# Rotary step: the exchanged halves copied by ScalarE, one VectorE operation fewer

## The reference, cut to what matters

```python
def _rope(x, pos):
    ang = pos[:, None] * inv[None, :]
    x1, x2 = x[..., :half], x[..., half:]
    return concatenate([x1 * cos - x2 * sin, x2 * cos + x1 * sin])
```

## Time and profile before

| what | value |
|---|---|
| median of 3 runs | 2270.43 us (2269.36 to 2271.97) |
| profiled execution | 2269.12 us, its span 2267.3 us |
| busy: TensorE, VectorE, ScalarE, GpSimd | 2232.9, 1803.7, 984.7, 990.3 us |
| attention halves, P k0 to the last output tile | from 40, 285.5, 1163 and 1400.3 us; 218.4, 209.2, 210.0 and 209.2 us long |
| feed-forward stretches | about 500 to 1145 and 1615 to 2250 us |

### The profile page before, as it was taken

One profiled execution on the slowest core, in us unless ns is written; L12 is line 12 of the kernel. 1 busy time (PEld: TensorE's weight loads), 2 busy tenths in 40 slices (PEclk: granted clock), 3 DMA queues, 4 the chain that ended last, 5 costly groups with the idle time before them and its releaser, 6 DMA issues.

```text
span 2267.3 us, 31231 instructions
## 1 busy us (share of the span) xinstructions
PE 2232.9 (98%) x10610; PEld 1858.7 (82%) x10610; DVE 1803.7 (80%) x2793; ACT 984.7 (43%) x1876; POOL 990.3 (44%) x686
## 2 busy tenths in 40 slices
PE   8999999999999999999999999999999999999998
PEld 6888888888888888888888888888888888888886
DVE  7998388888787878999958873988877676779988
ACT  4556144554444444443324541455444434444342
POOL 4314100124777777798700010001254455568893
PEclk9999999999999999999999999999999999999999
DMA  8633542233676766853243136312323232357522
GB/s 306 221 111 124 205 174 94 83 141 117 215 239 215 236 216 235 316 175 108 99 149 112 56 130 214 121 59 110 135 84 111 97 111 97 111 212 261 165 72 84
DMA packets 93463, 346.89 MB, mean 153 GB/s; under 512 B 9760, under 2 KB 9888, under 8 KB 74016
## 3 DMA queue, kind: packets, MB, share of 16 engines
q1 hardware_dynamic: 92624, 344.53, 43.7%
q10 hardware_dynamic: 720, 0.86, 0.1%
HBM read 237.35 MB, written 108.00 MB: 152 GB/s over the span
## 4 chain that ended last, share of the span: by engine, by line
PE 87%; DVE 6%; issue 1%; ACT 1%; POOL 0%; DVEq 0%; ACTq 0%; POOLq 0%
PE bank L528 28%; PE bank L530 27%; PE bank L529 27%; PE bank L1177 2%; PE bank L1015 1%; DVE x L2234 1%; DVE u L2200 1%; PE bank L1023 1%; PE bank L535 1%; PE bank L534 1%; DVE qpe L1928 1%; DVE aT_lo L2053 1%; DVE y_out L2341 0%; ACT aT_hi L1490 0%; DVE x L2242 0%
## 5 line engine op out<-in xcount | busy, mean ns | idle before, releaser
L905 POOL TENSOR_TENSOR slot<-raw,slot 128x512 fp32r<-128x512 f32 x160 | 223.4, 1400 | 234.4 <-ACT slot L1629 234.4
L528 PE MATMUL bank<-h_hi,slot 128*128 128x512 f32 x640 | 249.2, 389 | 0.0
L529 PE MATMUL bank<-h_lo,slot 128*128 128x512 f32 x640 | 249.1, 389 | 0.0
L530 PE MATMUL bank<-h_hi,slot 128*128 128x512 f32 x640 | 249.1, 389 | 0.0
L882 POOL TENSOR_TENSOR acc<-sq,zero 128x512 f32<-128x512 f32 x5 | 6.1, 1219 | 528.3 <-ACT sq L1418 528.3
L528 PE MATMUL bank<-u,slot 128*128 128x512 f32 x560 | 218.6, 390 | 1.1 <-DVE x L2234 1.1
L529 PE MATMUL bank<-u,slot 128*128 128x512 f32 x560 | 218.1, 389 | 0.0
L530 PE MATMUL bank<-u,slot 128*128 128x512 f32 x560 | 218.0, 389 | 0.0
L528 PE MATMUL bank<-h_hi,w 128*128 128x512 f32 x512 | 203.6, 398 | 0.0
L905 POOL TENSOR_TENSOR slot<-s_stage,slot 128x512 fp32r<-128x512 f32 x120 | 175.8, 1466 | 60.1 <-ACT slot L1629 58.6
L530 PE MATMUL bank<-h_hi,w 128*128 128x512 f32 x512 | 200.0, 391 | 0.0
(11 more groups left out here) (261 smaller groups left out, 5931.6 us busy)
## 6 DMA issues: line engine op xcount, KB each, us to landing
w<-parked SPq DMA_DIRECT2D x81, 1024.0 KB, 4.9
raw<-in_wffn SPq DMA_DIRECT2D x112, 512.0 KB, 3.5
u_kept<-made SPq DMA_DIRECT2D x148, 256.0 KB, 2.8
uf<-u_kept SPq DMA_DIRECT2D x70, 512.0 KB, 5.7
parked<-w SPq DMA_DIRECT2D x27, 1024.0 KB, 6.3
parked<-p SPq DMA_DIRECT2D x27, 1024.0 KB, 4.9
raw<-in_watt SPq DMA_DIRECT2D x27, 512.0 KB, 4.3
praw<-in_watt SPq DMA_DIRECT2D x27, 512.0 KB, 5.8
```

The source lines that it names most:

```text
L528: nc.tensor.matmul(out_ap, lhs[0], rhs[0], start=first, stop=False, skip_group_check=joins)
L529: nc.tensor.matmul(out_ap, lhs[0], rhs[1], start=False, stop=False, skip_group_check=joins)
L530: return nc.tensor.matmul(out_ap, lhs[1], rhs[0], start=False, stop=last, skip_group_check=joins)
L905: nc.gpsimd.tensor_tensor(slot[i][:, 1, :], gate_source(i), slot[i][:, 0, :].bitcast(F32), ALU.subtract).then_inc(s_gate_lo.sem, 1)
```

## The change

ScalarE gets a new item RS x in its order, which copies the two 64-partition halves of the projected tile from PSUM into the other halves of r2. It waits for the projection of the tile and for the end of the rotary step before it. VectorE waits for both copies, multiplies by the cosine table, multiplies all of r2 by the sine rows in place, and subtracts (the sine rows of partitions 64 to 127 hold the negative, so the sign changes). The bank counts as read after that product.

```diff
 SCALAR_ORDER = order("""
-    V | RH q0 | RH k0 | EX 0 | EX 1 | RH q1 | TH 0 | EX 2 | TH 1 | RH k1 | EX 3 | TH 2 | EX 4 | RH q2 | EX 5 | TH 3 |
-    YC 0 | TH 4 | RH k2 | EX 6 | RH q3 | TH 5 | EX 7 | TH 6 | EX 8 | RH k3 | TH 7 | EX 9 | EX 10 | SH y0 | TH 8 |
...
+    V | RS q0 | RH q0 | RS k0 | RH k0 | RS q1 | EX 0 | EX 1 | RH q1 | TH 0 | EX 2 | RS k1 | TH 1 | RH k1 | EX 3 |
+    RS q2 | TH 2 | EX 4 | RH q2 | EX 5 | TH 3 | YC 0 | RS k2 | TH 4 | RH k2 | EX 6 | RS q3 | RH q3 | TH 5 | EX 7 |
+    RS k3 | TH 6 | EX 8 | RH k3 | TH 7 | EX 9 | RS kpe | EX 10 | SH y0 | TH 8 | YC 1 | TH 9 | EX 11 | LC ckv | TH 10 |
...
+    PH kn0 | TH 14 | RS pe0 | PH qn0 | TH 15 | RH pe0 | EX 16 | PH vm0 | PH vm1 | PH vm2 | YC 3 | PH vm3 | PH kn1 |
+    SH y2 | EX 17 | TH 16 | PH qn1 | EX 18 | EX 19 | SQ 0 | PH kn2 | SQ 1 | TH 17 | SH y3 | EX 20 | RS pe1 | SQ 2 |
...
+            def swap_halves(l, b, name):
+                z = bank[TILE[name] % 2]
+                act.wait_ge(s_mm.sem, s_mm.half_at(l, b, DV_MM + TILE[name]))
+                act.wait_ge(s_roped.sem, s_roped.half_at(l, b, ROPED[name] - 1))
+                nc.scalar.activation(r2[0:64, :], z[64:128, :], ACT.Copy).then_inc(s_swapped.sem, 1)
+                nc.scalar.activation(r2[64:128, :], z[0:64, :], ACT.Copy).then_inc(s_swapped.sem, 1)
...
+                dve.wait_ge(s_swapped.sem, s_swapped.half_at(l, b, 2 * ROPED[name] + 1))
                 nc.vector.tensor_tensor(r1[:], z[:], tab[:, 0, :], ALU.mult)
-                nc.vector.tensor_tensor(r2[0:64, :], z[64:128, :], tab[64:128, 1, :], ALU.mult)
-                nc.vector.tensor_tensor(r2[64:128, :], z[0:64, :], tab[0:64, 1, :], ALU.mult).then_inc(s_rope_read.sem, 1)
+                nc.vector.tensor_tensor(r2[:], r2[:], tab[:, 1, :], ALU.mult).then_inc(s_rope_read.sem, 1)
                 dve.wait_ge(s_rope_read.sem, s_rope_read.half_at(l, b, ROPED[name]))
-                nc.vector.tensor_tensor(r1[:], r1[:], r2[:], ALU.add).then_inc(s_roped.sem, 1)
+                nc.vector.tensor_tensor(r1[:], r1[:], r2[:], ALU.subtract).then_inc(s_roped.sem, 1)
```

More of the change, by code:

```diff
@@ L83 @@
 SCALAR_ORDER = order("""
-    V | RH q0 | RH k0 | EX 0 | EX 1 | RH q1 | TH 0 | EX 2 | TH 1 | RH k1 | EX 3 | TH 2 | EX 4 | RH q2 | EX 5 | TH 3 |
-    YC 0 | TH 4 | RH k2 | EX 6 | RH q3 | TH 5 | EX 7 | TH 6 | EX 8 | RH k3 | TH 7 | EX 9 | EX 10 | SH y0 | TH 8 |
[L86 to L92, removed]
+    V | RS q0 | RH q0 | RS k0 | RH k0 | RS q1 | EX 0 | EX 1 | RH q1 | TH 0 | EX 2 | RS k1 | TH 1 | RH k1 | EX 3 |
+    RS q2 | TH 2 | EX 4 | RH q2 | EX 5 | TH 3 | YC 0 | RS k2 | TH 4 | RH k2 | EX 6 | RS q3 | RH q3 | TH 5 | EX 7 |
+    RS k3 | TH 6 | EX 8 | RH k3 | TH 7 | EX 9 | RS kpe | EX 10 | SH y0 | TH 8 | YC 1 | TH 9 | EX 11 | LC ckv | TH 10 |
+    EX 12 | RH kpe | SH y1 | TH 11 | EX 13 | EX 14 | SH ckv | LC cq0 | LC cq1 | TH 12 | EX 15 | TH 13 | SH cq | YC 2 |
+    PH kn0 | TH 14 | RS pe0 | PH qn0 | TH 15 | RH pe0 | EX 16 | PH vm0 | PH vm1 | PH vm2 | YC 3 | PH vm3 | PH kn1 |
+    SH y2 | EX 17 | TH 16 | PH qn1 | EX 18 | EX 19 | SQ 0 | PH kn2 | SQ 1 | TH 17 | SH y3 | EX 20 | RS pe1 | SQ 2 |
+    TH 18 | PH qn2 | RH pe1 | PH kn3 | EX 21 | TH 19 | PH qn3 | EX 22 | EX 23 | EX 24 | TH 20 | YC 4 | EX 25 | EX 26 |
+    TH 21 | TH 22 | EX 27 | TH 23 | TH 24 | SQ 3 | SQ 4 | YC 5 | TH 25 | EX 28 | TH 26 | EX 29 | EX 30 | SQ 5 | SQ 6 |
+    TH 27 | SQ 7 | SN 0 | TH 28 | SN 1 | SN 2 | TH 29 | EX 31 | SN 3 | SN 4 | SN 5 | TH 30 | YC 6 | TH 31 | YC 7 |
+    SN 6 | SN 7
 """)
@@ L456, in encoder_trunk @@
         s_roped = Count(sem("roped"), len(ROPED))
+        s_swapped = Count(sem("rope_halves_swapped"), 2 * len(ROPED))
         s_rope_hi = Count(sem("rope_hi"), len(ROPE_SPLITS))
@@ L1387, in _ @@
         def _(act):
-            for c in (s_plain_hi, s_rope_hi, s_latent, s_exp, s_at_hi, s_oc, s_ym_hi, s_sq, s_t_hi, s_x_hi, s_silu, s_u_hi, s_hi, s_a_hi,
+            for c in (s_plain_hi, s_swapped, s_rope_hi, s_latent, s_exp, s_at_hi, s_oc, s_ym_hi, s_sq, s_t_hi, s_x_hi, s_silu, s_u_hi, s_hi, s_a_hi,
                       s_gate_hi, s_snap, s_tx_hi):
@@ L1558, in _ @@
                                                      scale=rstd[:, m:m + 1]).then_inc(s_plain_hi.sem, 1)
+                        elif kind == "RS":
+                            swap_halves(l, b, what)
                         elif kind == "RH":
```

## The result

The kernel after takes 2286.77 us (median of 4 runs, 2285.64 to 2287.84) against 2270.37 us for the kernel before on the same chip: ratio 1.0070, 95% interval 1.0054 to 1.0086, or 16.4 us more. The forecast was 2273.5 us, range 2268.5 to 2277.8.

A forecast was written before the change was run, and what follows sets the result against it. TensorE, busy 98%, bounds the kernel. First half 2.0 - 0.2 + 0.4 = 2.2 us, later halves 3 x 0.3 = 0.9: 3.1 us more than the median 2270.43, so 2273.5 us; range 2268.5 to 2277.8.

The forecast's parts named there:

- 2.0 us for a step: Rotary step on VectorE: new step 0.60 + 0.70 + 0.69 = 2.0 us against 2.8 us, 0.8 us saved.
- a chance of 0.34: Whole kernel: chance given to slower by more than 0.2%; same had 0.60, faster 0.06.
- Its own sign of being wrong: Wrong if TensorE's waits for VectorE shrink, the first half shortens, or later halves grow by over 1 us each.
- The copies come early (k3) or just in time (pe0, pe1): Steps k3, pe0, pe1: end 0.8 us early or about as before; VectorE then waits for other things, nothing gained.
- So all 2.0 us goes to TensorE, the 1.2 included.: First half: lateness through k1, q2, k2, q3 costs TensorE 2.0 us by transposes 6, including 1.2 us at exponentials 4.
- 6.17: First half: copy-out of output 0 to q3 step's start takes 6.17 us, as in a later half; step starts at 93.0.
- kpe, called absorbed: Later halves: kpe late by about as much as q2, absorbed by VectorE's wait for transposed part 9; otherwise some 1 us.
- Between the 1.0 us of the earlier trace won and a loss of like size I take 0.2 us won.: First half's start: the k0 wait won against weight round 6 moved 2.4 us behind q0's copies; net 0.2 us won.
- I take 0.3 us in each of the three later halves.: Later halves: k2's late copies delay q3 and the combination for transposes 6; 0.2 us wait and refill, 0.3 us each.
- q1 was costed at nothing: Later halves: q1's step ends 0.3 us late, but VectorE idles before the next score, so cost is nothing.
- 0.4 us: First half: subtractions and sine products meeting GpSimd; four steps on the path bear 4/11 of 1.05 us, 0.4 us.
- dear hand-over: Rival: copy pair takes 1.34 us, ten path steps lose 0.24 us more each; 5.5 us, 2275.9 us; chance 0.29.

The follow-up runs named there:

- SQ 2 moved: The changed kernel with ScalarE's square that feeds GpSimd's addition moved from behind the copies of pe1 to behind the high parts of pe1; 2285.82 us, ratio 1.0061.
- copies moved ahead: The changed kernel with copies of k1, q2, k2, kpe, pe1 earlier on ScalarE, that square later, weight round 6 earlier, round 11 later; 2271.45 us, ratio 1.0002.
- k1 and q2 ahead: The changed kernel with copies of k1 ahead of exponentials 2, those of q2 ahead of exponentials 3, round 11 behind exponentials 3; 2284.74 us, ratio 1.0062.
- k2 ahead: The changed kernel with only the copies of k2 moved ahead of the copy-out of output 0 on ScalarE; 2284.58 us, ratio 1.0060.
- copies with old operations: The changed kernel keeping copies and VectorE's wait for them, but with the old four VectorE operations, which overwrite r2; 2308.58 us, ratio 1.0173.
- moved ahead with four old: The run with copies moved ahead, but q0, k0, q1 and q3 keep the old four-operation step; 2271.36 us, ratio 1.0002.
- chosen steps only: The changed kernel with copies only for k0, k1, q2, k2, k3, kpe, pe0 (k1, q2, k2, kpe moved ahead), old step elsewhere; 2270.31 us, ratio 0.9996.
- round 6 ahead: The changed kernel with only round 6 of the weights put ahead of the copies of q0 on ScalarE; 2285.51 us, ratio 1.0063.

## Why the prediction was wrong

Right: what bounds the kernel; that VectorE's saving by itself is worth nearly nothing; that copies standing behind late ScalarE work are what costs; the places k1, q2, k2 and, in the later halves, transposes 6; 2.0 us for a step. That it would be measurably slower had a chance of 0.34 only. Its own sign of being wrong came: the later halves grew by over 1 us each, so lateness reached TensorE where the forecast had it absorbed. Wrong:

1. *"The copies come early (k3) or just in time (pe0, pe1): the step ends 0.8 us early or about as before."* For pe1 this is false: the copies stand behind exponentials 20, which in the kernel before end (417.86) when the step already starts (417.91). It ends 0.5 us late, and VectorE's low part of output 3 behind it is wanted by oa0 at once. With GpSimd's 1.0 us, which the copies caused by holding up the square, that is 1.5 us in each later half, 4.5 us in all; the run with SQ 2 moved splits it.

2. *"So all 2.0 us goes to TensorE, the 1.2 included."* It was 4.1 us: 1.8 at scores 5 and 2.3 from scores 7 to transposes 6. The chain by k1, q2, the copy-out, k2 and q3 was right, the 1.2 us passed on to the copy-out included; three terms were too small. At k1 and q2 together 0.65 us more were lost, and from the copy-out's end to the start of the q3 step it took 6.81 us and not 6.17: the hand-over, some 0.3 us dearer at each of the four. Behind q3 the small operation that met GpSimd took 0.85 us more. And this lateness reaches TensorE at scores 8, by way of maxima and exponentials 7, just ahead of transposes 6. The two runs with one or two pairs of copies moved show that the waits add up: without the lateness of k1 and q2 2.3 us stay, without that of k2 1.9. A term of nothing was wrong besides: kpe, called absorbed, adds the 0.6 us at scores 11, which are gone in the run with its copies moved ahead.

3. *"Between the 1.0 us of the earlier trace rows won and a loss of like size I take 0.2 us won."* It was a loss of 1.4 us at scores 0 in the profiled execution, 2.6 us where the start was not late as well (the run with SQ 2 moved). By scores 1 it was 1.5 us there, and 3.1 us in each of the three runs that start alike and earlier (SQ 2 moved, k1 and q2 ahead, k2 ahead). The forecast followed round 6 to the load and round 8, but not GpSimd's part of it into the step of q0.

4. *"I take 0.3 us in each of the three later halves."* The mechanism was right, the term mis-sized: k2's lateness costs 0.96 us, part of it ahead of transposes 6 already, at scores 7 (behind exponentials 6) and transposes 5 (behind low part 4). The 0.65 us more are the hand-overs at k2 and q3: without the copy-out's own delay the q3 step ends 2.6 us late, where the forecast had 1.95. Scores 1 add 0.38 us, where q1 was costed at nothing behind VectorE's idle time: the idle time is there, but maxima 0 stand behind the step, and scores 1 need the bank that exponentials 0, behind these, read. Scores 5 add 0.16 us ahead of the wait that was to absorb it.

5. *"0.4 us"* for GpSimd, with 0.56 us as the most a meeting could cost. It takes 1.0 us, in 7 of the 44 subtractions (q0, k0, q1 and pe1 of the first half, pe1 of the others), and 1.1 us in q0's sine product. The Trainium skill (SBUF — State Buffer, Who interferes with whom) names a VectorE operation with two SBUF inputs beside a GpSimd operation that reads SBUF as a case of contention for the pair of ports that both share, and calls that pair an exclusive lock; the 1.67 us at pe1 agree. The worst row of the trace before (1.25 us) was only a meeting halfway: its subtraction started at 48.71, 0.60 us into a GpSimd operation of 1.30. Nor did the forecast look behind the step: the small operation L1878 after q3 takes 1.02 to 1.03 us in all nine profiles whose q3 has the short step, and 0.17 in the four where q3 keeps the four operations (the kernel before, copies with old operations, moved ahead with four old, chosen steps only).

The rival "dear hand-over" had the price nearly right: it asked for 0.24 us more at each of ten steps, and 0.30 us more (1.37 in place of 1.07) was measured at k2. That makes some 3 us, the hand-over terms of items 2 and 4, of a loss of 16. The rest is not its doing, and the run with the copies moved ahead has the same copies and loses nothing.

## What to carry to other kernels

Work that is moved to an engine with a fixed order is paid for by its place in that order, not by its length: the same 52 us of copies cost 16 us behind the wrong items and nothing measurable ahead of them. Lateness at two places adds up when TensorE has waited at the first, because the second is then counted from the delayed TensorE. And a shorter step puts its last operations at another time: look at what runs on GpSimd then, and whether both operands lie in SBUF.

## What the hardware showed that was not expected

- Two copies of 64 partitions into the other half start 0.62 us apart, with 0.59 us each: they don't overlap, where two operations on the same 128 partitions do, 0.48 us apart.
- A wait of TensorE is not always paid once. In the run with round 6 ahead a wait of 1.86 us at scores 5 was followed by a granted clock of 0.50, that is 1.2 GHz, and the projection behind it ended another 0.92 us late; in the kernel after, a wait of 1.82 us at the same item left the clock at 1.00, 2.4 GHz. First the run with round 6 ahead, then the kernel after:

```profile
78.00:80.00 2.00, 2.00 (x6) 1.52 (x6) 1.95 (x4) 1.76 (x5) 0.00 (x0) 0.50 1.03 428
```

```profile
82.00:84.00 2.00, 1.52 (x7) 1.25 (x8) 1.93 (x6) 2.00 (x6) 0.00 (x0) 1.00 1.00 383
```

- The clock also falls in some profiles ahead of the first rotary step, where the kernels don't differ. The first projection ended between 38.98 and 43.36 us in the thirteen profiles; in the kernel after at 42.56, behind a stretch from 30 to 36 us at a mean granted clock of 0.72, in the kernel before at 39.51. These 3.1 us of the profiled execution are not the change's, and a spread of this size in every kernel is why the runs that take away 1 to 5 us are told apart by their rows and not by their times. Whether the clock falls at a given wait in most executions stays open: each kernel has one profile.
